# Expert blocks in two sizes, 128 and 64 rows, in a routed expert layer on one core

## What is computed

```python
def moe(h, w_router, router_bias, w1, w3, w2, ws1, ws3, ws2):   # 64 experts, 8 per token, width 256
    scores = sigmoid(t @ w_router)                              # t: 256 tokens x 1024
    _, eidx = top_k(scores + router_bias, 8)
    g = take(scores, eidx); g = g / sum(g) * 2.5
    ...                                                         # tokens sorted by expert, blocks of 128
    def expert_block(args):                                     # for each block of one expert e
        xb = t[toks]
        return (silu(xb @ w1[e]) * (xb @ w3[e])) @ w2[e] * gs[:, None]
    routed = segment_sum(out, row_tok)                          # each token gets the sum of its 8 experts
    return routed + swiglu(t, ws1, ws3, ws2)                    # and the shared expert
```

## Time and profile before

| | us |
|---|---|
| median of three runs | 1058.93 |
| lowest and highest | 1056.66 and 1059.56 |
| span of the profiled execution | 1053.0 |
| TensorE busy | 1003.7 (95%) |
| VectorE busy | 787.6 (75%) |
| ScalarE busy | 584.7 (56%) |
| GpSimd busy | 287.9 (27%) |

### The profile page before, as it was taken

The page is one execution under the profiler, slowest core; times in us unless marked ns, Lnnn a source line. Parts: engine busy times, 40 slices in busy tenths (PEclk is TensorE's granted clock), DMA queues, the critical chain, the costliest instruction groups (busy, mean ns, idle before and its releaser), DMA issues. The chain is left out here.

```text
span 1053.0 us, 16530 instructions
## 1 busy us (share of the span) xinstructions
PE 1003.7 (95%) x5182; PEld 810.2 (77%) x5182; DVE 787.6 (75%) x1310; ACT 584.7 (56%) x895; POOL 287.9 (27%) x355
## 2 busy tenths in 40 slices
PE   8999999999999899989879989999999999999996
PEld 7778777778766676778768876778888888888885
DVE  4677888768844543566775654899999999999997
ACT  4554664445433342435425423777777777777774
POOL 5154452224100000041226113322322232233222
PEclk9999999999999999999989999999999999999999
DMA  9877777768635243536242316888888888788884
GB/s 315 277 260 257 225 237 274 234 201 283 211 99 180 96 160 120 171 93 232 88 153 88 101 60 259 313 307 321 341 327 313 334 332 329 306 340 341 325 314 179
DMA packets 85349, 247.39 MB, mean 235 GB/s; under 512 B 13276, under 2 KB 23957, under 8 KB 71986
## 3 DMA queue, kind: packets, MB, share of 16 engines
q1 hardware_dynamic: 71042, 201.19, 53.3%
q0 software_dynamic: 13680, 45.13, 12.0%
q10 hardware_dynamic: 576, 0.41, 0.1%
HBM read 244.27 MB, written 2.29 MB: 234 GB/s over the span
## 5 line engine op out<-in xcount | busy, mean ns | idle before, releaser
L1804 PE MATMUL bank<-w_hi,a_hi 128*128 128x512 f32 (+2 forms) x512 | 205.3, 401 | 10.0 <-DVE w_lo L1266 4.5
L1804 PE MATMUL bank<-w_hi,a_lo 128*128 128x512 f32 (+2 forms) x512 | 196.5, 384 | 0.0
L1804 PE MATMUL bank<-w_lo,a_hi 128*128 128x512 f32 (+2 forms) x512 | 196.2, 383 | 0.0
L1266 DVE TENSOR_TENSOR w_lo<-ring,w_hi 128x1024 fp32r<-128x1024 f32 (+2 forms) x132 | 152.7, 1181 | 50.4 <-ACT w_hi L989 46.5
L989 ACT ACTIVATE w_hi<-ring 128x1024 fp32r<-128x1024 f32 (+2 forms) x140 | 141.0, 1023 | 73.9 <-PE bank L1804 70.2
L1642 DVE TENSOR_TENSOR up_lo<-raw_weights,up_hi 128x1024 fp32r<-128x1024 f32 x136 | 164.4, 1250 | 3.0
L1149 ACT ACTIVATE up_hi<-raw_weights 128x1024 fp32r<-128x1024 f32 x136 | 135.8, 1050 | 0.1
L1804 PEld LDWEIGHTS bank<-w_hi,a_hi 128*128 128x128 f32 x512 | 96.2, 188 | 39.4 <-issue 17.6
L1804 PEld LDWEIGHTS bank<-w_hi,a_lo 128*128 128x128 f32 x512 | 96.2, 188 | 19.8
L1804 PEld LDWEIGHTS bank<-w_lo,a_hi 128*128 128x128 f32 x512 | 96.4, 188 | 18.2 <-issue 1.4
L2074 PE MATMUL bank<-up_hi,x_block_hi 128*128 128x512 f32 x264 | 105.1, 398 | 1.0 <-issue 1.0
(11 more groups left out here) (264 smaller groups left out, 1926.5 us busy)
## 6 DMA issues: line engine op xcount, KB each, us to landing
raw_weights<-in_w_dram SPq DMA_DIRECT2D x102, 1024.0 KB, 7.0
ring<-in_w_in_dram SPq DMA_DIRECT2D x58, 1024.0 KB, 5.8
merged<-in_w_ada_dram POOLq DMA_DIRECT2D x96, 256.0 KB, 4.2
ring<-in_w_out_dram SPq DMA_DIRECT2D x8, 1024.0 KB, 5.9
ring<-in_w_branch_dram SPq DMA_DIRECT2D x6, 1024.0 KB, 4.9
bias<-rel_rows SPq DMA_DIRECT2D x40, 128.0 KB, 5.2
block_rows<-place_rows SPq DMA_DIRECT2D x34, 128.0 KB, 8.7
ring<-in_ws_dram SPq DMA_DIRECT2D x2, 1024.0 KB, 5.3
```

Of the source, the lines that this page charges most:

```text
L1266: dve.tensor_tensor(w_parts[1][:, 2 * p:2 * p + 2, 0:w], view(JOB[it[1:3]], kind)[:, 2 * p:2 * p + 2, :], w_parts[0][:, 2 * p:2 * p + 2, 0 ...
L1804: mm = pe.matmul(ps[:, 0:wide], a_parts[za][:, k, t * P:(t + 1) * P], w_parts[zw][:, k, 0:wide], start=start, stop=stop)
```

## The change

The list of blocks now has two kinds. Even places take experts with more than 64 tokens, odd places those with up to 64; whichever kind is more numerous fills on (small ones also in even places; an odd place with no small expert is an empty block). A candidate's place is worked out from two counts, `large` and `small`, in four small operations. In an odd block the stationary tile holds the high parts of 64 rows beside their low parts (`xe_hi[:, :, 0:64]` and `[64:128]`), so that two products per weight tile (by high and by low weight) give all four partial products; the two halves of the result are added (`hsum`: ScalarE copies the lower half, VectorE adds) ahead of silu. In the down products the halves are not added: `put` sends row n and row 64+n to the same token. `put` is now made from the block's token column (`tok_f`) and a table of token numbers loaded once (`slots`), and the way over DRAM (`ranks` turned, `prow`, `place_rows`, `load_places`) falls away. In an odd block both scatters stand ahead of the turning of h, and the gather fetches 64 rows. The title's last part, all subtractions on VectorE, changes nothing here: they are there already (`UP_PIECES` lists the same four pieces in the same order).

```diff
+HALF = P // 2
+UP_PIECES = ((0, 0), (0, 1), (1, 0), (1, 1))
...
             load_down(0, load_up(0, 0))
             n_work = sp.value_load(work[0:1, 0:1], min_val=0, max_val=MAX_WORK)
-            sp.wait_ge(S("places_stored"), 16)
-            sp.wait_ge(S("token_columns"), NT)
-            load_places(0, 0)
+            sp.wait_ge(S("token_columns"), NT + 1)
+            load_columns(2, 2)
...
-                        gp.wait_ge(S(f"row_loaded_{r}"), 16 * (m4 + 1))
-                        gp.sem_inc(S("pool_begun"), 1)
-                        gp.tensor_scalar(put[:, :], row4[:, r, :], consts[:, C_COL:C_COL + 1], None, ALU.is_equal)\
+                        gp.sem_inc(S("begun"), 1)
+                        gp.tensor_scalar(put[:, :], slots[:, S_TOK:S_TOK + TOK], tok_f[:, r, 0:1], None, ALU.is_equal)\
...
+                        if r % 2:
+                            act.wait_ge(S("up_done"), i + 1)
+                            act.activation(hsum[0:HALF, :], hidden_b[HALF:P, :], ACT.Copy).then_inc(S("half_low_copied"), 1)
+                            act.wait_ge(S("half_summed"), m4 * (BODY // 2) + (r // 2 + 1))
+                            gated = hsum[0:HALF, 0:ED]
...
+                    chain(dve.tensor_scalar(used_at[:, 0:1], small, 1.0, n_large, ALU.add, ALU.min))
+                    chain(dve.tensor_tensor(used_at[:, 0:1], used_at[:, 0:1], small, ALU.add))
+                    chain(dve.scalar_tensor_tensor(out=used_at[:, 1:2], in0=large, scalar=2.0, in1=used_at[:, 0:1],
+                                                   op0=ALU.mult, op1=ALU.subtract))
+                    chain(dve.scalar_tensor_tensor(out=used_at[:, 1:2], in0=used_at[:, 1:2], scalar=kinds[:, 0:1],
+                                                   in1=used_at[:, 0:1], op0=ALU.mult, op1=ALU.add))
...
-                    dve.wait_ge(S("ranks_turned"), 1)
-                    dve.tensor_copy(prow[:, :], y_b[0][:, 0:TOK]).then_inc(S("rows_turned"), 1)
...
+                dve.tensor_copy(tok_f[:, r, :], hidden_b[:, 2:3]).then_inc(S("gates_ready"), 1)
...
+                if half:
+                    dve.wait_ge(S("half_low_copied"), pair(0) + 1)
+                    dve.tensor_tensor(hsum[0:HALF, :], hidden_b[0:HALF, :], hsum[0:HALF, :], ALU.add)\
+                       .then_inc(S("half_summed"), 1)
                 dve.wait_ge(S("silu_done"), i + 1)
-                dve.tensor_tensor(he, hs[:, 0, :], hidden_b[:, ED:2 * ED], ALU.mult).then_inc(S("h_done"), 1)
-                rest_of_rows(i + 1)
+                dve.tensor_tensor(he[0:rows], hs[0:rows, 0, :], (hsum if half else hidden_b)[0:rows, ED:2 * ED], ALU.mult)\
+                   .then_inc(S("h_done"), 1)
+                rest_of_rows(nxt, pair(1))
...
-                    for n, (zx, zw) in enumerate(PASSES):
+                    passes = PASSES[0:2] if half else PASSES
+                    for n, (zx, zw) in enumerate(passes):
...
                     pe.wait_ge(S("put_ready"), i)
                     scatter(0, i)
+                    if half:
+                        scatter(1, i).then_inc(S("block_done"), 1)
                 pe.wait_ge(S("h_done"), i + 1)
...
+                if half:
+                    pe.wait_ge(S("h_lo_ready"), i + 1)
                 for hf in range(2):
...
+                    passes = DOWN_PASSES[0:2 * FT] if half else DOWN_PASSES
+                    for n, (f, zh, zw) in enumerate(passes):
+                        if not half and hf == 0 and n == 2 * FT:
                             pe.wait_ge(S("h_lo_ready"), i + 1)
```

More of the change, by code:

```diff
@@ L512, in build @@
         ranks = sb("ranks", [P, NT, NV], F32, routing)
-        prow = sb("prow", [NV, TOK], F32, routing)
         gsum = sb("gsum", [P, NT], F32, routing)
         used = sb("used", [NV, 1], F32, routing)
-        place = sb("place", [NV, 1], F32, routing)
+        kinds = sb("kinds", [NV, 2], F32, routing)
+        used_at = sb("used_at", [NV, 2], F32, routing)
+        place = sb("place", [NV, 4], F32, routing)
+        n_blocks = sb("n_blocks", [1, 1], F32, routing)
         order = sb("order", [NV, NV], F32, routing)
@@ L1655, in _, with expert_block @@
             take_tokens(1, 1)
-            for kh in range(2):
-                for m in range(2):
-                    rest_of_up_weights(0, 0, kh, m)
-            rest_of_rows(0)
-            dve.wait_ge(S("work_ready"), 2)
+            for kh, m in UP_PIECES:
+                rest_of_up_weights(0, 0, kh, m)
+            rest_of_rows(0, 0)
+            dve.wait_ge(S("work_ready"), 3)
             n_work = dve.value_load(work[0:1, 0:1], min_val=0, max_val=MAX_WORK)
-            def expert_block(i, r):
+            def expert_block(i, r, pair):
                 nxt = (r + 1) % BODY
+                half = r % 2
+                rows = HALF if half else P
                 for f in range(FT):
@@ L1693, in _ @@
                     with dve.If(n_work > i):
-                        expert_block(i, (b + 1) % BODY)
+                        expert_block(i, (b + 1) % BODY,
+                                     lambda d: turn * (LONG // 2) + (part * (BODY // 2) + (b + 1 + d) // 2))
             for hf in range(2):
@@ L2025, in _ @@
             pe.wait_ge(S("router_exp"), 1)
[L2026 removed]
+            pe.matmul(y_b[1][:, 0:2], tri, kinds[:, :], start=True, stop=True)
+            pe.matmul(y_b[1][:, 2:4], ones[:, :], kinds[:, :], start=True, stop=True).then_inc(S("places_counted"), 1)
             up(wv, 0, 1, range(2, 6))
[L2028 to L2031 removed]
             pe.wait_ge(S("order_ready"), 1)
             pe.matmul(y_b[1][0:1, 0:NV], consts[:, C_EXP:C_EXP + 1], order[:, :], start=True, stop=True)
[L2034 to L2035 removed]
+            pe.matmul(y_b[1][0:1, NV:2 * NV], consts[:, C_PLACE:C_PLACE + 1], order[:, :], start=True, stop=True)\
               .then_inc(S("list_product"), 1)
@@ L2047, in turn_rows @@
                 pe.wait_ge(S(f"rows_gathered_{r}"), 16 * loads)
+                if r % 2:
+                    pe.sem_inc(S("begun"), 1)
+                    for k in range(KT):
+                        mm = pe.transpose(y_b[0][:, k * HALF:(k + 1) * HALF], xg[0:HALF, r % 2, k * P:(k + 1) * P],
+                                          consts[0:HALF, C_ID:C_ID + HALF])
+                    mm.then_inc(S("half_rows_turned"), 1)
+                    return
                 for q in range(2):
@@ L2085, in expert_block @@
                     scatter(0, i)
+                    if half:
+                        scatter(1, i).then_inc(S("block_done"), 1)
                 pe.wait_ge(S("h_done"), i + 1)
+                rows = HALF if half else P
+                if half:
+                    pe.sem_inc(S("begun"), 1)
                 for f in range(FT):
-                    mm = pe.transpose(turned_b[:, f * P:(f + 1) * P], he[:, f:ED:FT], ident)
+                    mm = pe.transpose(turned_b[:, f * rows:(f + 1) * rows], he[0:rows, f:ED:FT], consts[0:rows, C_ID:C_ID + rows])
                 mm.then_inc(S("h_turned"), 1)
-                if not first:
+                if not first and not half:
                     scatter(1, i).then_inc(S("block_done"), 1)
@@ L2095, in expert_block @@
                 pe.wait_ge(S("down_lo"), 2 * i + 2)
+                if half:
+                    pe.wait_ge(S("h_lo_ready"), i + 1)
                 for hf in range(2):
-                    pe.wait_ge(S(f"x_lo_ready_{hf}"), i + 2)
-                    for n, (f, zh, zw) in enumerate(DOWN_PASSES):
-                        if hf == 0 and n == 2 * FT:
+                    if half:
+                        pe.wait_ge(S(f"x_lo_ready_{hf}"), pair(1) + 1)
+                    elif hf == 0:
+                        pe.wait_ge(S("half_x_lo_ready"), pair(1) + 1)
+                    passes = DOWN_PASSES[0:2 * FT] if half else DOWN_PASSES
+                    for n, (f, zh, zw) in enumerate(passes):
+                        if not half and hf == 0 and n == 2 * FT:
                             pe.wait_ge(S("h_lo_ready"), i + 1)
@@ L2132, in _ @@
                     with pe.If(n_work > i):
[L2133 removed]
+                        expert_block(i, (b + 1) % BODY,
+                                     lambda d: turn * (LONG // 2) + (part * (BODY // 2) + (b + 1 + d) // 2),
+                                     turn * (LONG // BODY) + (part + (1 + (b + 2) // BODY)))
             pe.wait_ge(S("put_ready"), n_work)
```

159 lines of the change are left out of this document (91 added, 68 removed).

## The result

The change made the kernel slower by about 9 us. In runs that alternated on one chip the median went from 1059.08 us (four runs, 1056.66 to 1059.56) to 1068.07 us (four runs, 1067.43 to 1068.98), a ratio of 1.009 with the interval 1.007 to 1.011. That is beyond the 0.3% that a measurement of this kernel can tell, and inside the range of the prediction, seven above its 1061. One of the four executions of `again` (3277.59 us) and one of the twelve of `early_gap` (1128.87) ran in a slow state; they count in the medians further down but not in the ratios, and without its one `again` has 1067.90.

The account below looks back on a forecast made before the run. TensorE bounded the kernel, VectorE 7% behind; the changed odd block was a ring through VectorE. Head +1.2 and block terms (-0.1, +0.6, +0.3, -0.1) made +1.9, span 1054.9; 5.9 more gave 1061, range 1050 to 1074.

Parts of the forecast that it names:

- The bound and the walk: Expert stage: TensorE bound, VectorE 7% behind; walking an odd and even block gave 23.35 us per pair.
- the odd block's ring: Odd block: closed chain from rounding and `down_hi` through VectorE's sum, silu and `h_lo` to down products, 11.9 us.
- The terms taken between bounds: Odd block: estimated VectorE operations, the sum 0.65 us, token copy 0.12, `h_lo` 0.29.
- The page against the row: Turning 64 rows on TensorE: 0.23 us by the skill's formula, 0.65 by the trace row's excess; hidden behind `he`.
- The head: Routing ahead of block 0: extra small operations on the path cost +1.2 us (0.6 to 1.8).
- block 0 near 658: Start of the expert stage: block 0 starting near 658 us would show the routing estimate of +1.2 us right.
- The median is 5.9 above the span: Whole kernel: median 1058.93 against the profile's span of 1053.0, added to the forecast span of 1054.9.
- Rival C: Odd blocks: idle TensorE loses clock; every second one paying 1.7 us is +13, 1074; chance 0.14.
- the forecast's case: Expert stage: pair of blocks between 23.0 and 23.7 us; chance 0.48.
- the window 348 to 351: Earlier trace: TensorE busy 1.36 of 3 us at full clock, held against idle time costing clock.
- Freed DMA time has no buyer: DMA queues: removing the row broadcast and halving odd gathers gains nothing, as no weight is waited for.
- Rival B: Even gather decides: at 7.9 us, 0.45 per pair, +7, 1068; sign, idle beyond 2 us before turning; chance 0.19.

Follow-up runs that it names:

- again: The kernel after the change, run once more unchanged: 1068.60 us, ratio 1.0102 to the kernel before.
- early_gap: Changed kernel, one `up_hi` and `up_lo` behind silu, odd scatters first, gather ahead of `put`, unused products (six before turning, two before finding tokens): 1059.24 us.
- no_sum: Changed kernel without ScalarE's copy of the low half and VectorE's sum in odd blocks: 1051.28 us, ratio 0.9947.
- products_only: Kernel before with only 16 up and 8 down products in odd blocks, waiting for `h_lo` before the down products: 1054.27 us, ratio 0.9973.
- put_alone: Kernel before, all blocks of 128 rows, with `put` made from the token column and the way over DRAM removed: 1053.53 us, ratio 0.9946.
- before_again: The kernel before the change, run once more unchanged: 1057.98 us, ratio 1.0006.
- fill: Changed kernel plus products without a use in odd blocks, 7 ahead of turning the rows and 5 ahead of finding tokens: 1060.10 us, ratio 1.0027.
- scatter_first: Changed kernel with both scatters of an odd block ahead of the turning of the gathered rows: 1093.79 us, ratio 1.0342.
- early_fill: Changed kernel, odd blocks: one `up_hi` and one `up_lo` moved behind silu and tokens, scatters first, nine products without a use: 1055.69 us, ratio 0.9978.

## Why the prediction came out as it did

**The bound and the walk: right.** The forecast rested on the odd block's ring, not on the product count, and the ring is what the chain of waits shows. In us from the place where the prediction put its zero, the change of the chain from down to up products (809.51 in the earlier trace rows, 743.97 = 741.08 + 2.89 here, 0.18 after the first up product of the list in order of time):

| step | predicted | measured |
|---|---|---|
| turning of the gathered rows starts | 5.5 | 4.65 (748.62) |
| sum starts | 6.26 | 6.24 (750.21) |
| silu starts | 6.95 | 6.95 (750.92) |
| `x_block_lo` starts | 8.03 | 8.02 (751.99) |
| `h_lo` done | 9.62 | 9.51 (753.20 + 0.28) |
| down products start | 9.75 | 9.80 (753.77) |
| next up products | 11.9 | 11.93 (753.77 + 2.13) |
| even block | 11.5 | 11.52 |

`no_sum` confirms the ring by shortening it, and `products_only` that the saved products are worth 3 us of 45. The terms taken between bounds held: the sum 0.67 (0.65 taken), `h_lo` 0.28 (0.29), the pair at full clock 23.45 (23.35). Two readings in the sum were 0.16 us late and of no effect: block 5 starts at 716.54 and block 31 at 1018.38.

**The page against the row: the row.** Turning eight pieces of 64 rows takes 0.64 us in the chain of waits above (738.03), against 0.91 for 128 in the earlier trace rows. The prediction's row with its excess kept on top gave 0.65; from the unrounded 0.91 that sum is 0.70, so that the exact agreement is luck. The formula of the Trainium skill, "TensorE: Matmul & The Clock Gate", section "Back-to-back issue gap", which the section gives for an isolated product and calls too low for short ones in a stream, gave 0.23; the trace disagrees with that value for this stream. The term was hidden behind `he` either way.

**The head: right.** From the reciprocal to the last entry of the work list it was 11.00 us before (627.38 to 638.38) and 12.13 after (632.16 to 644.29): +1.1, for +1.2. The sign given for it, block 0 near 658, did not come (662.34): 4.8 us of that are the chance ahead of the router.

**"The median is 5.9 above the span": wrong, and harmless.** A run's time is 1.9 us above its span in every profile but that of `put_alone`, where it is 2.3. The other four were chance in the first execution of before, as `before_again` shows. The sum survived only because it was applied as a difference, and that is luck.

**The clock: the step that failed.** Rival C was described with its right place (idle ahead of the turning and ahead of the down products) and very nearly its right price for one block (1.7 us for 1.5), but it stood at 0.14 as an alternative to the forecast, at eight blocks or none. The sum of the forecast had nothing for it. It came on top of the forecast's case instead, in four of sixteen blocks in one trace and five in the other: 6 to 7 us in the stage, 7 to 8 in the median, by `fill`. The evidence set against it was the window 348 to 351 of the earlier trace rows, a stretch with a low share and a full clock. That row says only that one idle stretch was forgiven. 16 odd blocks are 16 chances, and two idle stretches close together with nothing but turnings between them are another pattern, as `scatter_first` shows with 33 us at an unchanged busy share. The Trainium skill, same page, section "Loop structure matters more than you think", holds that the loop's waits decide it; the traces of this case agree, with 0.98 after, 0.90 in `scatter_first` and 1.00 in `fill`.

**"Freed DMA time has no buyer": wrong, by 2 us in the stage.** The prediction asked for waits for weights and found none; but the stage of before does wait for gathers, 17 times, and with the broadcast gone they are there in time. By `put_alone` removing the way over DRAM is worth 2.0 us of the stage and 5 of the whole. If the parts simply add, which no run shows, the two sizes as they are cost the sum of both: about 9 us of slowdown and 5 of gain that they used up, 14 to 15 in all. By that account 7 to 8 of them are the clock, and the rest is the longer odd block (0.38 us each, 6 in all) and the head's 1.1.

**Rival B** was given 1068, which is what was measured, and that is a coincidence. It did not decide the block that was followed, since the gather landed 0.8 us earlier than walked (6.34 us from issue to turning for 7.14); TensorE waited 0.93 us for it there, where over 2 was named as the sign. The mechanism was the next bound behind the ring: it capped `no_sum` and `products_only`, and `early_fill` in part.

## What to carry to other kernels

Before counting removed products as time, follow one iteration through the queue of the second-busiest engine: where that engine closes a ring, work removed elsewhere only turns into waiting, and operations added to the ring are paid in full. Then ask where the new waiting lies on TensorE, since idle stretches in the wrong place can cost more than the removed work gave, and a few products without a use, put where no operand is ready, or another order buy it back. Time each part of a change with several parts by itself: here the plainest one was worth as much as the best form of the whole.

## What the runs showed of the hardware

- TensorE's clock depended on where the idle time lay, not on its sum: busy 290.61 and 290.77 of 323 us, granted 0.98 and 0.90, with waits of 2.38 and 2.39 us in one odd block. In the lost stretches it was 0.50, that is 1.2 GHz, and 512-column products started 0.43 us apart for 0.23.
- The same idle pattern in the same code lost the full level in 4 of 16 odd blocks in one execution and in 5 in the other, and only in part in the same ones.
- Two executions of the same code were 4 us apart by 627 us, with more time at the half clock in the later one (some 17 us for 7), so that two spans are better compared from the last untouched instruction on.
